# Gate projections moved into the attention steps, and the next layer's modulation beside the first projections

## The reference, cut to what matters

```python
shift, scale, gate = split(silu(c) @ w_mod[l] + b_mod[l], 3)       # w_mod[l]: 1024 x 3072
h = rms_norm(x, g_pre[l]) * (1 + scale) + shift
z = h @ w_in[l]                       # 11 groups of 512 columns, then 3072 merge logits
o_ret  = heads(rms_norm(bidir_retention(rq, rk, rv))) * silu(rg)
o_diff = heads(rms_norm(diff_attend(dq, dk, dv))) * silu(dg)
o_mlp  = mu * spatial_mix(layer_norm(mv)) * silu(mg)
g_ret, g_mlp, g_diff = split(sigmoid(merge_logits), 3)
out = (g_ret * (o_ret @ w_bo[0]) + g_mlp * (o_mlp @ w_bo[1]) + g_diff * (o_diff @ w_bo[2])) @ w_o
x = x + gate * rms_norm(out, g_post[l])
```

## Time and profile before

| | us |
|---|---|
| runs: median (lowest, highest) | 2080.15 (2077.9, 2083.12) |
| profiled execution: span from first to last instruction | 2081.5 |
| PE / POOL / ACT / DVE busy | 1949.3 / 1368.9 / 1095.3 / 595.7 |

### The profile page before, as it was taken

The page is one execution under the profiler, slowest core; times in us unless marked ns, Lnnn a source line. Parts: engine busy times, 40 slices in busy tenths (PEclk is TensorE's granted clock), DMA queues, the critical chain, the costliest instruction groups (busy, mean ns, idle before and its releaser), DMA issues.

```text
span 2081.5 us, 26149 instructions
## 1 busy us (share of the span) xinstructions
PE 1949.3 (94%) x9524; PEld 1569.8 (75%) x9524; DVE 595.7 (29%) x1123; ACT 1095.3 (53%) x1571; POOL 1368.9 (66%) x573
## 2 busy tenths in 40 slices
PE   6998999998899979989989999999999989999997
PEld 3776887776668768767878777788888867788886
DVE  3214303424303262351226121331112532132111
ACT  3545644445534654465455685554445586555443
POOL 2755687854558668447869644488887844468884
PEclk8999999999999999999999999999999999999999
DMA  9643465543576536335646433256554633345653
GB/s 343 204 136 121 134 191 171 172 121 112 184 263 209 178 112 192 102 90 172 189 129 184 143 92 101 98 178 192 181 190 138 200 94 96 106 142 174 189 181 112
DMA packets 170816, 328.66 MB, mean 158 GB/s; under 512 B 12384, under 2 KB 13536, under 8 KB 170464
## 3 DMA queue, kind: packets, MB, share of 16 engines
q1 hardware_dynamic: 167968, 320.49, 50.0%
q10 hardware_dynamic: 2752, 6.84, 0.9%
HBM read 326.24 MB, written 1.05 MB: 157 GB/s over the span
## 4 chain that ended last, share of the span: by engine, by line
PE 42%; issue 29%; POOL 25%; ACT 3%; POOLq 1%; DVE 1%; DMA 0%; DVEq 0%; ACTq 0%
POOL wlo L467 25%; PE G L1435 9%; PE G L1437 9%; PE G L1436 9%; PE A L1435 3%; PE A L1437 3%; PE A L1436 3%; ACT whi L481 1%; PE A L1489 1%; ACT t L547 1%; PE A L1817 0%; PE A L1816 0%; PE A L1815 0%; ACT L843 0%; PE G L1877 0%
## 5 line engine op out<-in xcount | busy, mean ns | idle before, releaser
L467 POOL TENSOR_TENSOR wlo<-raw,whi 128x1024 fp32r<-128x1024 f32 x568 | 1365.2, 2411 | 690.0 <-ACT whi L481 686.0
L481 ACT ACTIVATE whi<-raw 128x1024 fp32r<-128x1024 f32 x568 | 599.5, 1058 | 677.5 <-PE G L1437 554.5
L1435 PE MATMUL G<-whi,hhi 128*128 128x512 f32 (+1 forms) x1648 | 662.5, 402 | 21.5 <-DVE hlo L949 9.3
L1437 PE MATMUL G<-whi,hlo 128*128 128x512 f32 (+1 forms) x1648 | 645.2, 392 | 0.0
L1436 PE MATMUL G<-wlo,hhi 128*128 128x512 f32 (+1 forms) x1648 | 644.7, 391 | 0.0
L1435 PEld LDWEIGHTS G<-whi,hhi 128*128 128x128 f32 x1648 | 313.8, 190 | 103.1 <-issue 28.8
L1437 PEld LDWEIGHTS G<-whi,hlo 128*128 128x128 f32 x1648 | 313.4, 190 | 66.5
L1436 PEld LDWEIGHTS G<-wlo,hhi 128*128 128x128 f32 x1648 | 314.3, 191 | 60.1
L1435 PE MATMUL G<-whi,ohi 128*128 128x512 f32 x240 | 94.9, 396 | 1.9 <-ACT gates L494 1.4
L1436 PE MATMUL G<-wlo,ohi 128*128 128x512 f32 x240 | 93.7, 390 | 0.0
L1437 PE MATMUL G<-whi,olo 128*128 128x512 f32 x240 | 93.5, 390 | 0.0
(11 more groups left out here) (360 smaller groups left out, 2262.7 us busy)
## 6 DMA issues: line engine op xcount, KB each, us to landing
raw<-in_w_in SPq DMA_DIRECT2D x332, 512.0 KB, 3.7
raw<-in_w_up SPq DMA_DIRECT2D x64, 512.0 KB, 3.7
raw<-in_w_down SPq DMA_DIRECT2D x64, 512.0 KB, 3.5
raw<-in_w_out SPq DMA_DIRECT2D x40, 512.0 KB, 4.0
raw<-in_w_branch_out SPq DMA_DIRECT2D x36, 512.0 KB, 4.3
modw<-in_w_mod SPq DMA_DIRECT2D x32, 512.0 KB, 3.9
raw<-in_w_branch SPq DMA_DIRECT2D x24, 512.0 KB, 3.5
modz<-in_w_mod SPq DMA_DIRECT2D x16, 512.0 KB, 11.2
```

Source lines behind the costliest of these rows:

```text
L467: pool.tensor_tensor(wlo[:, s], raw[:, s], whi[:, s].bitcast(F32), ALU.subtract).then_inc(lo_ready, 1)
L481: act.activation(whi[:, slot], raw[:, slot], ACT.Copy).then_inc(hi_ready, 1)
L1435: pe.matmul(bank, hi, whi[:, slot, kk, 0:n], start=first, stop=False)
L1437: return pe.matmul(bank, lo, whi[:, slot, kk, 0:n], start=False, stop=last)
```

## The change

The merge logits join the late list, which then has 44 slabs (11 chunks, banks G2/G3). Two slabs stand in each retention step, two behind the scores and one behind the transposes in each difference step, eight after the spatial product, and the last two among the transposes of the branches. ACT copies the logits raw into columns of `z` that are dead by then (`GATE_HOMES`) and applies sigmoids in place; the gate of MG gets its SiLU in place too. `y` of the merge stands in RG and DG of `z`, the output of the projection moves to another buffer, and the value products use G0 and G1. The 24 slabs of layer 1's w_mod stand beside the last four dense chunks of pass 0 (16) and beside the second and third chunk of pass 1 (8); their six rows are kept in two new buffers, and are turned in one go in the fourth chunk of pass 1. Nothing in the second block is changed but the name of one buffer and the banks passed as an argument.

```diff
 sync (DMA order), one full pass
-                    for c, col in enumerate([RK, RQ, DKc, DQ]):
+                    beside = (range(3, 3 + 6 * SLOTS), range(3 + SLOTS, 3 + 3 * SLOTS), (), ())[n]
+                    for c, col in enumerate([RK, RQ, DKc, DQ, RV, DV] + LATE):
                         for s in range(SLOTS):
                             slab(flat["w_in"], l * D + s * SLAB_K * P, col, s)
-                            if n == 0 and 3 <= c * SLOTS + s < 3 + 2 * SLOTS:
+                            if c * SLOTS + s in beside:
                                 mod_slab()
...
                     for c in range(3 * D // CH):
...
-                            if n == 1 and c * SLOTS + s >= 2:
-                                mod_slab()
+                        chunk(flat["w_in"], l * D, MG + W + c * CH)
 lists
         LATE = [MV, RG, DG, MU, MG]
-        LATE_DIFF = 4 * SLOTS - (H1 + 1) - H1 * TT
+        GATE_HOMES = [RK, RQ, DKc, DQ, RV, DV]
+        Y_HOMES = [RG, DG]
+        LATE_SLABS = (len(LATE) + len(GATE_HOMES)) * SLOTS
 scalar
+                if n == 0:
+                    mod_copy(A[2], modkept[0])
+                if n == 1:
+                    mod_copy(A[1], modkept[5])
...
-                for i in range(H1 + 1):
-                    late_slab(i, late_dst)
+                for i in range(2 * (H1 + 1)):
+                    late_slab(i, late_dst, G[2:4])
...
-                act.wait_ge(late_evacuated, w(late_evacuated, 4 * TT))
-                for c in (RG, DG):
+                act.wait_ge(late_evacuated, w(late_evacuated, len(LATE) * TT))
+                for c in (RG, DG, MG):
                     act.activation(z[:, :, c:c + W], z[:, :, c:c + W], ACT.Silu).then_inc(gates_ready, 1)
-                while late < len(LATE) * SLOTS:
-                    late_slab(late, late_dst, ACT.Silu)
+                while late < LATE_SLABS - 2:
+                    late_slab(late, late_dst, G[2:4])
                     late += 1
+                def sigmoid(c):
+                    home = z[:, :, GATE_HOMES[c]:GATE_HOMES[c] + W]
+                    act.activation(home, home, ACT.Sigmoid).then_inc(gates_ready, 1)
+                act.wait_ge(late_evacuated, w(late_evacuated, 5 * TT))
+                for c in (0, 2, 4, 1, 3):
+                    sigmoid(c)
+                highs = [ap for b in range(3) for ap in two_kt(ohi[:, b], 4)]
+                split_high(highs[0:4])
+                late_slab(late, late_dst, G[2:4])
+                split_high(highs[4:6], 4)
+                late_slab(late + 1, late_dst, G[2:4])
                 act.wait_ge(late_evacuated, w(late_evacuated, TT))
-                split_high([ap for b in range(3) for ap in two_kt(ohi[:, b], 4)])
+                sigmoid(5)
...
-                for c in range(3 * D // CH):
-                    evacuate(c % 2, columns(gates, c * CH), ACT.Sigmoid)
-                    if n == 1:
-                        mod_copy(A[c % 2], moddrop[:, c % 2])
 tensor, projections
                     pe.wait_ge(evacuated, w(evacuated, TT))
+                    if n == 1 and c == 1:
+                        pe.wait_ge(x_updated, w(x_updated))
                     for s in range(SLOTS):
                         slab(G[2 * c:2 * c + 2], hhi, hlo, s, fresh=c == 0, ready=rope_in if is_x else projected)
                         if n == 0:
                             mod_slab(A[2 + c])
+                        if n == 1 and c == 1:
+                            mod_slab(A[0])
...
+                            if n == 1 and c == 0:
+                                mod_slab(A[1])
+                            if n == 1 and c == 1 and s == 1:
+                                pe.wait_ge(mod_copied, w(mod_copied, 2))
+                                for b in range(6):
+                                    mod_turn(A[2], 8 * b, modkept[b], b == 5)
                 else:
-                    with w.loop(2, pair_counts(2)) as i:
...
+                    for c in range(4):
+                        pe.wait_ge(evacuated, w(evacuated, TT))
+                        if c >= 2:
+                            pe.wait_ge(mod_copied, w(mod_copied))
+                        for s in range(SLOTS):
+                            slab(G[2 * (c % 2):2 * (c % 2) + 2], hhi, hlo, s)
+                            mod_slab(A[2 + c % 2])
                 pe.wait_ge(evacuated, w(evacuated, 2 * TT))
-                if n == 1:
-                    pe.wait_ge(x_updated, w(x_updated))
+                if n < 2:
+                    pe.wait_ge(gate_ready, w(gate_ready))
                 if n == 0:
+                    pe.wait_ge(mod_copied, w(mod_copied, 2))
 tensor, heads
-                    late_slab(i)
+                    for b in range(2):
+                        late_slab(2 * i + b, G[2:4])
...
-                        late_slab(late)
-                        late += 1
+                        for _ in range(2):
+                            late_slab(late, G[2:4])
+                            late += 1
...
-                        if j < LATE_DIFF:
-                            late_slab(late)
-                            late += 1
+                        late_slab(late, G[2:4])
+                        late += 1
...
-                while late < len(LATE) * SLOTS:
-                    late_slab(late)
+                while late < LATE_SLABS - 2:
+                    late_slab(late, G[2:4])
                     late += 1
                 pe.wait_ge(branches_ready, w(branches_ready, 3))
-                turn_branches()
-                pe.wait_ge(late_evacuated, w(late_evacuated, TT))
...
-                for c in range(3 * D // CH):
-                    pe.wait_ge(evacuated, w(evacuated, TT))
-                    for s in range(SLOTS):
-                        slab(G[2 * (c % 2):2 * (c % 2) + 2], hhi, hlo, s)
...
+                turn_split(branch_tiles(BRANCH_KS[0:8]), settle=False)
+                late_slab(late, G[2:4])
+                turn_split(branch_tiles(BRANCH_KS[8:12]), 4, settle=False)
+                late_slab(late + 1, G[2:4])
```

More of the change, by code:

```diff
@@ L219, in build @@
         gate2_5 = sb("gate2_5", [P, TT, CH])
+        modkeep = sb_at("modkeep", [P, 4, MODN], F32, place["gate2_5"])
+        modlast = sb("modlast", [P, 2, MODN])
+        modkept = [modkeep[:, m] for m in range(4)] + [modlast[:, m] for m in range(2)]
         modT = sb("modT", [P, 2, KT, 2])
@@ L503, in pass_by, with late_slab @@
                 split(SLOTS - 1)
-            def late_slab(n, dst, func=ACT.Copy, scale=None):
+            def late_slab(n, dst, banks, scale=None):
                 c, s = divmod(n, SLOTS)
@@ L512, in late_slab @@
                         act.wait_ge(late_projected, w(late_projected))
-                        act.activation(dst[c][t], G[t][:], func, scale=1.0 if scale is None else scale[t])\
+                        act.activation(dst[c][t], banks[t][:], ACT.Copy, scale=1.0 if scale is None else scale[t])\
                            .then_inc(late_evacuated, 1)
@@ L1030, in rotate, with merge @@
                 return dve.tensor_tensor(x2, c, d, ALU.add)
-            def merge(in_first, then_norm=None, next_mod=False):
+            def merge(gate, part, then_norm=None):
                 split_low([ap for b in range(3) for ap in two_kt(ohi[:, b], 4)],
@@ L1466, in late_slab @@
                     pe.wait_ge(late_evacuated, w(late_evacuated, TT))
-                slab(G[0:2], hhi, hlo, s, ready=late_projected)
+                slab(banks, hhi, hlo, s, ready=late_projected)
             def turn_heads(blocks):
@@ L1507, in pair_counts, with branch_tiles @@
                 return {lo_ready.name: SLOTS * n, evacuated.name: TT * n}
-            def turn_branches():
-                turn_split([lambda t, b=b, k=k: o[:, b, t, k * P:(k + 1) * P] for b in range(3) for k in range(4)], settle=False)
+            def branch_tiles(ks):
+                return [lambda t, b=b, k=k: o[:, b, t, k * P:(k + 1) * P] for b, k in ks]
+            BRANCH_KS = [(b, k) for b in range(3) for k in range(4)]
             mods = {"n": 0}
@@ L1537, in mod_turn, with merge @@
                     ins.then_inc(mod_turned, 1)
-            def merge(ready, next_mod=False, gate=None):
+            def merge(ready, y, gate=None, late_bank=False):
                 for u in range(6):
                     b = u % 3
-                    if u in (1, 2) and not next_mod:
+                    if u in (1, 2):
                         pe.wait_ge(split_lo, w(split_lo, 2))
+                    if u == 1 and late_bank:
+                        pe.wait_ge(late_evacuated, w(late_evacuated, TT))
                     for s in range(2):
@@ L1558, in merge @@
                             ins.then_inc(weights_used, 1)
-                    if u == 0 and next_mod:
-                        mod_turn(A[2], 40, moddrop[:, 1])
                     if u == 4:
-                        turn_split([lambda t, k=k: y[:, t, k * P:(k + 1) * P] for k in range(4)], settle=False)
```

(7 more changed lines are left out.)

106 lines of the change are left out of this document (47 added, 59 removed).

## The result

The changed kernel takes 2094.98 us (median of 4 runs, 2092.41 to 2096.24), the kernel before 2081.64 in the same comparison (2077.9 to 2085.57): ratio 1.0074, 95% interval 1.0056 to 1.0092. (The quotient of the two medians is 1.0064. The profiled execution took 2093.85 us, its span is 2092.1, that is 10.6 more than before, where the forecast's sum was +10.4. The total is right. The parts are less so, errors of both signs cancel, and the agreement to 0.2 us is luck.

The account below looks back on a forecast made before the run. The prediction took TensorE, busy for 94% of the span, to set the pace. Terms of -41.4 and +51.8 us summed to +10.4 on the profiled execution's 2081.5, less 1.35 to the runs' median: 2090 us, range 2079 to 2101.

Parts of the forecast that it names:

- mix and transposed-weight waits: Difference-attention steps: PE's waits for VectorE's mix and ACT's transposed weights would go, -20.8 us over three passes.
- branch wait: PE's wait for the branches would go: 2.02, 3.25 and 3.28 us in passes 0, 1 and 3.
- the one at 89.69: POOL's wait at 89.69 would go, as slabs beside w_mod are used more slowly: 1.10 + 0.14 us.
- rope wait: The rope wait at 384.10 would go: 1.63 + 0.14 us.
- A: Rival at chunk boundaries: evacuations are in time, 12.5 us of boundary waits fall away, 2078 us; chance 0.10.
- C: Rival in the difference-attention steps: DVE held by POOL, 2136 us, or 2113 if half; chance 0.06.
- D: Rival at the first projections: w_mod beside them starves, 2102 us if each of 24 lost 0.5; chance 0.05.
- B: Rival on PE's clock: it holds through the waits, 7.0 us less, 2083 us, no change; chance 0.14.
- Item 1: Late list's chunk boundaries: PE waits for both evacuations of one bank pair; with small matmuls +11.3 us, bounds 1.8 and 18.
- Item 2: After the difference attention: evacuation behind ACT's table loads and SiLUs delays slab 36, plus boundary 39|40; +8.4 us, bounds 3 and 12.
- Item 3: After slab 42: five sigmoids on ACT ahead of the branches' first high half make PE wait; 4.85 us a pass, 14.6 together.
- Items 4 and 5: Half clock behind the 4.25 us waits, +4.5 us; pass 1's second chunk waiting for x_updated, 8.2, clock 2.5, together +10.8.

Follow-up runs that it names:

- e8: Changed kernel with the squares of heads 0 to 2 taken one step earlier, only head 3 left for the end: 2088.10 us, ratio 1.0040.
- e2: Changed kernel with the five sigmoids one by one behind the splits of late slabs 36, 37, 39, 40 and 41: 2073.40 us, ratio 0.9976.
- e4: Kernel before with only the w_mod lines of the change: 2089.01 us, ratio 1.0061.
- e5: Changed kernel with pass 1's six turns one by one behind six slabs instead of in one block: 2087.71 us, ratio 1.0052.
- e11: Changed kernel run again, unchanged: 2094.76 us, ratio 1.0073 to the kernel before.
- e9: Changed kernel with early evacuation, single sigmoids, last w_mod slabs a chunk later, single turns, slabs 36 to 39 in the other banks: 2045.81 us, ratio 0.9837.

## Why the forecast came out

**Where it was right.** The balance, and the reason for the sign: waits of one form replaced by waits of another. The mix and transposed-weight waits of the head steps went (windows 165:213 and 472:532 have 1.77 and 2.66 idle for 7.8 and 7.1 in the earlier trace rows). The branch wait went, and the merge's first wait, the one at 89.69 and the rope wait. Rivals A (no boundary waits), C (VectorE starved in the head steps) and D (w_mod starves: from 400 to 410 us, beside such pairs, PE is busy for 10.00 of 10.00 us at 307 GB/s) did not happen. B (the clock holds) did not either.

**Item 1, single bank pair.** Forecast 9.5 without its small-matmul term; measured 0.69 x 2 + 0.47 x 2 and 0.05 in pass 0, 0.90 x 2 with 0.30 and 0.25 in passes 1 and 3: 7.1. The boundaries fell where the schedule put them.

**Item 2, the tail: the step that failed in size.** Forecast +5.4 for slab 36; measured 3 x 3.6 = 10.8, with the clock near or at half behind it in each pass (0.61, 0.59, 0.50), which I had not charged. The chain was right link by link, but I took the squares at the 1.22 us of the kernel before. In the changed order they start 0.12 us behind a low half of GpSimd and take 3.31, so 2.1 of the 3.59 are this one link, which e8 shows to be GpSimd's. I had the two rows for it, a VectorE operation that is 353 ns at best and 2216 at worst, and used them for rival C alone, not for the chain that was already late. Slab 40: 3 x 0.69 for 3.0. In all 12.9 for 8.4.

**Item 3, sigmoids.** Forecast 14.6 with restarts, the wait itself 4.25; measured 4.10, 4.01, 4.01. e2 shows it is the queue order alone.

**Items 4 and 5, clock and x_updated.** The clock was to cost 4.5 + 2.5 = 7.0, and busy time is up by 5.7 in all. The two don't measure the same: the forecast also took 5.4 of busy time away (transposes 4.0, spatial matmuls 1.4) and added 1.8 for small matmuls, so its own balance was +3.4 and some restarts. The clock fell in more places than I named. The wait was forecast at 8.2 and came as 6.77. e4 has 8.05: the forecast's chain is right for w_mod's half, and the difference is the table load that the other half of the change takes out of this chain. I costed the halves apart where one changes the table state that the other meets.

**Left out: the turns.** I wrote that the six turns stay six and charged nothing. They became one block of 48 in which the clock fell; e5 puts it at 4 to 5 us. So item 2 was 4.5 too low in waits, the turns were missed, and items 1, 3 and 5 together were 6.3 too high (restarts included); the sum hid it. That what is left comes to 0.2 us is luck: the second profiled execution of the changed kernel (e11) is 15.9 above the span before, not 10.6.

**The clock.** The granted clock is near half behind the 3.59 us wait (0.61), behind the 4.10 us wait (0.65), around the 6.77 us wait (0.50), and in the block of turns with the slab behind it (0.52), where PE was never idle. How long it stays low differs from place to place and from execution to execution: behind the wait before slab 36 of pass 1 the first matmul takes 0.50 us here and 0.80 in e11, and pass 1's busy time is 309.8 and 313.9. Removing nearly all of the waits and the block of turns does pay: e9's PE is busy for 19.2 us less than the changed kernel's with the same 9524 matmuls. The Trainium skill, "TensorE: Matmul & The Clock Gate", Part 1, has an idle TensorE at half rate, which fits the first three; it has no idle time to go by in the fourth. What made the clock fall there was not shown. What remains open is how much of a single edit's gain comes from its own effect on the clock and how much from chance: the single edits' busy times (1947.5 to 1958.0) don't order as their causes would.

## What to carry to other kernels

When products are moved from one end of a stage into its middle, the vector and scalar work that rode on them stays behind in one engine's queue: write out that queue in order, and look for a bank's evacuation or a split behind a wait for another engine. Split PE's span into idle and busy before comparing two kernels with the same matmuls: in two executions here idle time differed by 0.6 us and busy time by 5.9; the first shows waits, the second the clock. And cost the halves of a change together where they share a state, such as the activation table that is loaded.

## What the runs showed of the hardware

- VectorE's squares, a product of two operands in SBUF, waited out a running GpSimd operation: 128x128 of them took 2.31 us where the next took 0.28.
- The granted clock fell in the middle of a block of 48 matmuls of two columns while PE was busy throughout (0.11 us each, then 0.22).
- A table load took 1.28 us on ScalarE, with gaps of 0.01 to 0.02 around it, and with the load out of the chain a wait was 6.77 instead of 8.05.
